# Half of the output projection's inner dimension, multiplied during the threshold search

## The reference

```
sc = indexer_scores(q_idx, w_idx, k_idx)      # one score per query and key
_, idx = lax.top_k(sc, topk)                  # 256 keys per query are attended
a_out = attend(...)                           # 512 rows of the concatenation
s_out, p_out = ssd_mixer(...), pool_mixer(...) # 256 + 256 rows
mix = jnp.concatenate([a_out, s_out, p_out], axis=-1) @ w['w_out']   # 1024 x 1024
x = x + g1 * mix
```

## Time and profile before

| | |
|---|---|
| median of three runs | 3217.33 us |
| span of the profiled execution | 3218.5 us |
| TensorE busy | 3014.0 us, 94% |
| VectorE busy | 1604.0 us, 50% |
| ScalarE busy | 1334.5 us, 41% |
| GpSimd busy | 262.7 us, 8% |
| chain that ended last, by engine | PE 64%, DVE 6%, issue 3%, ACT 2% |
| layer 0's search, layer 1's search | 397 to 556 us, 1975 to 2129 us |
| layer 0's output projection, layer 1's | 761 to 860 us, 2329 to 2431 us |

### The profile page before, as it was taken

One profiled execution on the slowest core, in us unless ns is written; L12 is line 12 of the kernel. 1 busy time (PEld: TensorE's weight loads), 2 busy tenths in 40 slices (PEclk: granted clock), 3 DMA queues, 4 the chain that ended last, 5 costly groups with the idle time before them and its releaser, 6 DMA issues.

```text
span 3218.5 us, 56238 instructions
## 1 busy us (share of the span) xinstructions
PE 3014.0 (94%) x20185; PEld 2635.5 (82%) x20185; DVE 1604.0 (50%) x3493; ACT 1334.5 (41%) x2398; POOL 262.7 (8%) x334
## 2 busy tenths in 40 slices
PE   7999878889999999999989997889899999999998
PEld 5899433558999999999989963346599999999998
DVE  4565699764722322322556567986474222222234
ACT  4433688665522122122443247866564211211234
POOL 1012321011000000000000141100300000000000
PEclk8999989989999999999999998999899999999999
DMA  6622365026311111111432343620642111111124
GB/s 201 163 65 69 108 236 184 2 100 196 99 52 43 48 46 43 48 46 46 116 89 55 69 131 132 209 92 2 230 129 63 45 46 50 46 42 52 46 72 139
DMA packets 356491, 293.60 MB, mean 91 GB/s; under 512 B 85288, under 2 KB 319206, under 8 KB 356024
## 3 DMA queue, kind: packets, MB, share of 16 engines
q1 hardware_dynamic: 325036, 186.21, 19.8%
q0 software_dynamic: 31152, 104.76, 10.5%
q10 hardware_dynamic: 108, 0.11, 0.0%
HBM read 273.33 MB, written 9.78 MB: 88 GB/s over the span
## 4 chain that ended last, share of the span: by engine, by line
PE 64%; DVE 6%; issue 3%; ACT 2%; DMA 1%; POOL 0%; DVEq 0%; ACTq 0%; POOLq 0%; SPq 0%
PE bank L859 44%; PE bank L876 11%; PE bank L843 2%; DVE arena L2635 2%; PE bank L1436 1%; PE bank L1410 1%; DMA arena<-in_cache_v,page_idx 1%; PE bank L917 1%; ACT arena L1902 1%; DVE w_lo L2107 1%; PE bank L1241 0%; PE bank L1370 0%; PE bank L1499 0%; POOL arena L725 0%; ACT w_hi L1629 0%
## 5 line engine op out<-in xcount | busy, mean ns | idle before, releaser
L859 PE MATMUL bank<-h_hi,w_hi 128*128 128x352 f32 x2736 | 891.7, 326 | 11.7 <-DVE arena L2261 7.2
L859 PE MATMUL bank<-h_lo,w_hi 128*128 128x352 f32 x2736 | 880.0, 322 | 0.0
L859 PE MATMUL bank<-h_hi,w_lo 128*128 128x352 f32 x2736 | 879.2, 321 | 0.0
L2107 DVE TENSOR_TENSOR w_lo<-weights,w_hi 128x1024 fp32r<-128x1024 f32 x250 | 306.4, 1225 | 678.0 <-ACT w_hi L1629 671.5
L859 PEld LDWEIGHTS bank<-h_hi,w_hi 128*128 128x128 f32 x2736 | 515.9, 189 | 17.2 <-issue 13.7
L859 PEld LDWEIGHTS bank<-h_lo,w_hi 128*128 128x128 f32 x2736 | 516.5, 189 | 0.3
L859 PEld LDWEIGHTS bank<-h_hi,w_lo 128*128 128x128 f32 x2736 | 515.2, 188 | 0.0
L1629 ACT ACTIVATE w_hi<-weights 128x1024 fp32r<-128x1024 f32 x250 | 264.1, 1056 | 453.3 <-PE bank L859 294.6
L843 PEld LDWEIGHTS bank<-arena 128*128 128x128 f32 (+2 forms) x1717 | 199.3, 148 | 163.3 <-issue 95.3
L843 PE MATMUL bank<-arena 128*128 128x128 f32 (+2 forms) x1717 | 271.1, 290 | 46.1 <-ACT arena L1939 15.8
L876 PE MATMUL bank<-g_hi,w_hi 128*128 128x352 f32 (+2 forms) x768 | 255.7, 333 | 11.1 <-DVE arena L767 5.4
(11 more groups left out here) (396 smaller groups left out, 4369.6 us busy)
## 6 DMA issues: line engine op xcount, KB each, us to landing
arena<-in_w_ada SPq DMA_DIRECT2D x96, 512.0 KB, 4.5
weights<-in_w_down SPq DMA_DIRECT2D x48, 512.0 KB, 3.9
weights<-in_w_gate SPq DMA_DIRECT2D x44, 512.0 KB, 3.8
weights<-in_w_up SPq DMA_DIRECT2D x44, 512.0 KB, 3.8
weights<-in_w_in SPq DMA_DIRECT2D x66, 256.0 KB, 3.8
weights<-in_w_down SPq DMA_DIRECT2D x32, 448.0 KB, 3.6
weights<-in_w_out SPq DMA_DIRECT2D x96, 128.0 KB, 2.9
weights<-in_w_out SPq DMA_DIRECT2D x48, 256.0 KB, 3.1
```

Source lines behind the costliest of these rows:

```text
L859: mm = pe.matmul(bank[:, 0:TC], wt[:, w], xt[:, x], start=(k + m == 0), stop=(k == n_k - 1 and m == 2))
L2107: dve.tensor_tensor(w_lo[:, w], S(O_W + n % 2 * UNIT, UNIT), w_hi[:, w].bitcast(F32), ALU.subtract).then_inc(unit_lo, 1)
```

## The change

For the first two token blocks in layer 0, and the first in layer 1 (`EARLY`), the lower half of the projection (k = 4 to 7, scan and pooling) is multiplied inside the search, in fp32 and without splitting: one product of four matmuls, an output tile m and a token block c, at the end of TensorE's part of every odd pass, from pass 1 in layer 0 (16 products) and from pass 17 in layer 1 (8). SyncE loads the weights of a tile m (256 KB, one buffer) ahead of a pass's `w_ada`. VectorE adds the product to the stream in the next pass, right after its first count (and after `logits_in`, where that pass has it). In the projection the units of those blocks keep k = 0 to 3: two transfers, splits over 512 columns, 12 matmuls. Of the gates, tiles 4 to 7 are rounded only for the blocks that remain.

To make room, ring `A` has two banks in the search, and the outputs of the counts that nobody reads share two buffers per engine, with waits between the counts; key tiles are taken in pairs: in a pass one half of two tiles is transposed, and the two halves of the pass before are multiplied one after the other. The bias of the gate's modulation is added before the search in layer 0, at the first early product in layer 1.

```diff
@@ sizes and places
+EARLY = (2, 1)
+def early_at(l, i):
+    first = 1 if EARLY[l] == 2 else 17
+    if i < first or i % 2 == 0:
+        return None
+    q = (i - first) // 2
+    return q, q // EARLY[l], q % EARLY[l]
+
+def early_base(l):
+    return KD * EARLY[0] * l
-        O_KT = [R(18, 512 * n) for n in range(3)]
-        O_JUNK = R(18, 512 * 3)
+        O_KT = [R(18, 512 * n) for n in range(4)]
+        O_EARLY = R(18, 512 * 4)
+        O_JUNK = (R(18, 512 * 5), R(18, 512 * 5 + 528))
+        O_SIGNS = (R(9), R(18, 512 * 5 + 848))
@@ SyncE
+                def early_unit(m):
+                    if m:
+                        sp.wait_ge(early_done, early_base(l) + EARLY[l] * m)
+                    settle(sp)
+                    sp.dma_start(V(O_EARLY, [[P, 4], [1, P]]), wo[512:1024, m * P:m * P + P].rearrange("(i p) n -> p i n", p=P)).then_inc(early_full, 16)
                 for u in range(4 * KD):
+                    m, rest = divmod(u - (1 if EARLY[l] == 2 else 17), 2 * EARLY[l])
+                    if rest == 0 and m >= 0:
+                        early_unit(m)
                     if u > 1:
                         sp.wait_ge(w_empty, ada_base(l) + u - 1)
...
+                    unit(n, *heads, *(rest if u // KD >= EARLY[l] else ()))
@@ TensorE
-            def product_part(bank, n, x0, wide, hi, lo, used=False, tiles=None, first=0):
-                for k in range(KD):
+            def product_part(bank, n, x0, wide, hi, lo, used=False, tiles=None, first=0, n_k=KD):
+                for k in range(n_k):
...
-                A.restart()
+                A.use(AB_FEW)
...
-                    n, half = h // 2, h % 2
+                    n, half = s // 2 * 2 + j, s % 2
...
+                def key_logits(s):
+                    half = s % 2
+                    A.wait_read(A.count.n - evicted[s])
+                    for i in range(2):
+                        n = s // 2 * 2 + i
+                        gq, j = n // 16, n % 4
+                        if j == 0:
+                            logit_banks[half] = Dr.open()
+                        mm = pe.matmul(B(logit_banks[half], [[1, 512]], 0, 32 * j, 32), S(O_QB + 32 * (4 * gq + j), 32), S(O_KT[(2 * s + i) % 4], 512),
+                                       start=True, stop=True)
+                        if half == 0:
+                            mm.then_inc(s_kv_used, 1)
+                        elif j == 3:
+                            Dr.close_all(mm, 2)
+                def keys(s):
+                    for j in range(2):
+                        keys_turned(s, j)
+                    if s:
+                        key_logits(s - 1)
+                def early_product(i):
+                    if early_at(l, i) is None:
+                        return
+                    q, m, c = early_at(l, i)
+                    if c == 0:
+                        pe.wait_ge(early_full, (l * KD + m + 1) * 16)
+                    if early_base(l) + q:
+                        pe.wait_ge(early_read, early_base(l) + q)
+                    for k in range(4):
+                        mm = pe.matmul(GB[:, 0:TC], S(O_EARLY + P * k, P), S(H(4 + k, c * TC), TC), start=(k == 0), stop=(k == 3))
+                    mm.then_inc(early_done, 1)
                 for i in range(PASSES):
...
                     modulate(O_ADA[i % 2], i % (2 * KD) // 2, i % 2).then_inc(w_empty, 1)
+                    early_product(i)
                 keys(K_TILES - 1)
                 modulation_turn(KD + SEARCH_ROWS[l][1][0])
-                for h in (2 * K_TILES - 2, 2 * K_TILES - 1):
-                    key_logits(h)
+                key_logits(K_TILES - 1)
...
+                                              n_k=4 if c < EARLY[l] else KD))
@@ ScalarE
-                w = slice(n % 2 * UNIT, n % 2 * UNIT + UNIT)
+                w = slice(n % 2 * UNIT, n % 2 * UNIT + wide)
...
-                        junk = S(O_JUNK + 1296 + (S_OFF[j + 2] - S_OFF[5]) // 2, P * (j + 3) // 2).bitcast(BF16)
+                        junk = S(O_SIGNS[j % 2 == 0], P * (j + 3) // 2).bitcast(BF16)
+                        if j == 3:
+                            act.wait_ge(sign_counted, 3 * (l * PASSES + i) + 1)
...
-                split_hi(0, 3)
+                def out_unit(u):
+                    return (2, 4 * P) if u // KD < EARLY[l] else (3, UNIT)
+                split_hi(0, *out_unit(0))
...
-                for k in range(KD):
-                    gate_hi(k, 0, TC)
+                for k in range(4):
+                    gate_hi(k, 0, TC, 1 if k < 3 else KD - 3)
...
-                        gate_hi(k, TC, 2 * TC)
+                        gate_hi(k, *((TC, 2 * TC) if k < 4 else (EARLY[l] * TC, (3 - EARLY[l]) * TC)))
@@ VectorE
+                def early_added(i):
+                    if i < 0 or early_at(l, i) is None:
+                        return
+                    q, m, c = early_at(l, i)
+                    if l and q == 0:
+                        biased(2 * KD, KD)
+                    dve.wait_ge(early_done, early_base(l) + q + 1)
+                    x = S(O_X + m * TOK + c * TC, TC)
+                    dve.scalar_tensor_tensor(out=x, in0=GB[:, 0:TC], scalar=S(O_MOD + 9 * (2 * KD + m), 1), in1=x,
+                                             op0=ALU.mult, op1=ALU.add).then_inc(early_read, 1)
                 def tally(i, sets):
                     for j in sets:
...
+                        junk = S(O_JUNK[j % 2 == 0 and j < 6], n // 2).bitcast(BF16)
+                        if j == 1 and i:
+                            dve.wait_ge(count_raw, l * (PASSES + 1) + (i + 1))
+                        if j == 2:
+                            dve.wait_ge(dve_step, step.count.at(-1))
...
                             if i > 5 and i % 4 == 2:
                                 logits_in((i - 6) // 4)
+                            early_added(i - 1)
...
                 logits_in(7)
+                early_added(PASSES - 1)
...
-                    split_lo(u + 1)
+                    split_lo(u + 1, out_wide(u + 1) if u < 3 * KD - 1 else UNIT)
```

More of the change, by code:

```diff
@@ L875, in product_part @@
                     for m, (wt, xt) in enumerate(((w_hi, hi), (w_hi, lo), (w_lo, hi))):
-                        mm = pe.matmul(bank[:, 0:wide], wt[:, w], xt[:, x], start=(k + m == 0), stop=(k == KD - 1 and m == 2))
+                        mm = pe.matmul(bank[:, 0:wide], wt[:, w], xt[:, x], start=(k + m == 0), stop=(k == n_k - 1 and m == 2))
                         if used and k + m == 0:
@@ L1377, in keys @@
[L1377 to L1382 removed]
+                    evicted[s] = A.count.n
+                def key_logits(s):
[12 more added lines that the diff above has]
+                            Dr.close_all(mm, 2)
@@ L2850, in _, with out_wide @@
                 sample_rows(0)
-                split_lo(0)
-                for k in range(KD):
-                    gate_lo(l, 0, k, 0, TC)
+                def out_wide(u):
+                    return 4 * P if u // KD < EARLY[l] else UNIT
+                split_lo(0, out_wide(0))
+                for k in range(4):
+                    gate_lo(l, 0, k, 0, TC, 1 if k < 3 else KD - 3)
                 sample_rows(1)
```

67 lines of the change are left out of this document (27 added, 40 removed).

## The result

The changed kernel takes 3236.82 us, the median of five executions (3230.91 to 3242.76), against 3217.22 for the kernel before (3209.84 to 3218.4). The ratio is 1.0058, with a 95% interval of 1.0045 to 1.0071: it is slower, by 0.6%. I had said 3220, and 3211 to 3229 for the likeliest case. The wide range went to 3237, so the time lies inside it by 0.2 us. That is luck: the upper end was kept for rivals that did not come, and the forecast of "no change" was wrong by 17 us.

A forecast was written before the change was run, and what follows sets the result against it. TensorE was taken to bound most of the span, with VectorE close behind. Projection -25.5, search +27.5 and bias add +0.4 made +2.4 us: 3221 by the profiled span, stated as 3220 by the median; range 3203 to 3237.

The forecast's parts named there:

- Term -25.5: Projection, both layers: halved units shorten VectorE's turns to 2.66 us, gaining 16.5 us in layer 0 and 9.0 in layer 1.
- Rival 3: Projection: TensorE runs at 1.2 GHz through all short units, 21 us more, 3241; chance 0.05.
- Sum 17.6: Layer 0's search, first pass to last: VectorE's waits and adds, plus passes 1 and 17, cost 17.6 us.
- a wait above 2 us at the add: Search, even passes: forecast wrong if VectorE waits above 2 us at the add; 1.40 was expected in plain passes.
- +27.5: Search of both layers with its ends: early products and adds cost 19.8 us in layer 0 and 7.7 in layer 1.
- 4.5 less 2.2 for pass 1's product: Start of layer 0's search: pass 1's product at half clock costs some 4.5 us, of which 2.2 come back.
- End of the search: Each layer, after the last pass: selection starts 1.65 us later and the last add takes 0.5, 2.15 together.
- The edits costed at nothing: Search: waits for shared discarded-output buffers cost nothing; early weights land in time, with 1 to 2 us slack.
- Rival 1: Search: VectorE's add finds the product done, so the stalls of 14.8 us go, 3205; chance 0.20.
- Rival 2: Search: pairs don't overlap or modulation weights come late, product ends 0.87 us later, 19 more, 3239; chance 0.14.

The follow-up runs named there:

- run 1: Changed kernel with VectorE's add of an early product moved behind all four counts of the even pass, instead of behind the first; 3211.21 us.
- run 2: Changed kernel with only the key-tile pairs and their buffers: no early products in the search, full 24-matmul projection units; 3216.05 us.
- run 11: run 8 plus fourteen dummy fp32 matmuls on TensorE between products 7 and 8 of layer 1's projection; 3205.21 us.
- run 12: run 11 plus dummy matmuls in search passes without early product, four each, eight where logits are evicted; 3206.88 us.
- run 5: Changed kernel plus eight dummy fp32 matmuls on TensorE at the end of every search pass without early product; 3236.49 us.
- run 8: run 1 with layer 0's sixteen early products in a pass list starting at pass 3, so none in pass 1; 3210.28 us.
- Run 9: run 1 with key tiles taken one by one, as in the kernel before, instead of in pairs; 3227.87 us.
- run 10: run 8 with early products and shortened projection in layer 0 only; layer 1 keeps the pairs; 3210.34 us.
- run 7: Changed kernel with the early product placed between the transposes and the logits pair in odd passes; 3232.43 us.

## Why the prediction was right or wrong

**The number.** The forecast was 3220 and the time 3236.82. The forecast meant no change (+2.4), and the kernel became slower by 19.6; the range to 3237 held by 0.2 us only. What follows takes the sum behind the number term by term.

**Projection: right.** Term -25.5, measured -23.9 by the medians. Layer 0, unit 0 to 8: 31.5 before, 21.35 in run 1, forecast 20.7; to unit 16 63.43 and 47.40, 16.0 against 16.5. The changed kernel's own 23.3 is not an error of the turns: its product 0 ran at half clock (3.82 for 12 matmuls). That comes and goes between runs, in full units (65.9 in run 2) and short ones (49.2 in run 11) alike; what decides it I can't say: TensorE's last wait for a value gather was 2.23 us ahead of it in the changed kernel and 2.09 in run 11 (half clock), but 3.85 in run 12 (full). Rival 3 (half clock in all short units) did not come; in layer 1 one unit is hit, the first full-width one, and run 11 shows that its idle wait (3.53 us in the changed kernel) is the cause, worth 2.5 us.

**Search: the step that failed.** As the prediction put it, "In passes with an eviction ahead of the add VectorE comes at 6.48: 0.2 + 0.5 = 0.70. Layer 0 has seven of these (6, 10 to 30) and six plain" and "Sum 17.6". The count of passes and the price of an undisturbed one are right: 5.96 to 6.04, with an eviction or without, against 5.92 and 5.94. What was left out is that the stall itself and the pairs leave TensorE idle 2.3 us before the next count, and that a product at 1.2 GHz then meets VectorE. In the profiled execution passes 12, 14, 22 and 24 cost 14.8 over before, where I had 5.2: 9.6 more. The prediction named a wait above 2 us at the add as a sign that it was wrong, and passes 12, 22 and 24 show 4.51, 2.85 and 2.97. In run 5 these passes are plain ones. By medians the same fill brings nothing although it raises the clock of every execution, so how much of the 19 us between +27.5 and +46.7 is the clock's in an average execution stays open.

I had a rule for it in hand. "TensorE: Matmul & The Clock Gate" of the Trainium skill, section A second HAM failure mode, says that frequent micro-idles between groups of matmuls can make the clock swing. I weighed it against TensorE's pauses of before, 1.4 us at most, and placed it in the projection. After the change the pauses in the search are 2.3 us, and there the trace agrees (0.59, 0.72, 0.57, 0.66). A rule on idle time has to be held against the idle time that the change makes.

**Start of layer 0's search: under-sized.** I had 4.5 less 2.2 for pass 1's product. Passes 2 to 4, less the plain add in pass 4, cost 6.4: 4.1 more. What I had at nothing there is the key tiles' landing behind the early weights, 2.9 us more wait than before; run 8 takes 3.9 off pass 2.

**End of the search: right**, +2.6 and +2.2 against 2.15 each.

**The edits costed at nothing** cost nothing: run 2 has all the new waits for shared buffers and its passes take 4.03 and 5.23 as before. The early weights were on time for all 24 products of the changed kernel, pass 1's too; what they cost is the key tiles' landing at the start.

**Rivals.** Rival 1 (no wait) did not come, but run 1 is it, made by hand: I had 3205 for it, by the sum that mis-sized the rest, and it measured 3211. Rival 2's price (3239) is near the result, but not its mechanism: pairs do overlap. The four instructions of the pair (L1402) start at 448.35 and 448.80, two at a time, and are through by 449.40: 1.05 us, as long as the two instructions of one logits matmul alone. Run 9, which has no pairs and the late add, shows what their lack costs there, some 14 to 17 us.

## What to carry to other kernels

Work that is shifted into another engine's slack is paid for where its result is taken in, and the place of that step in the consumer's queue is a separate decision: one line, moved past 2.2 us of other work, turned +0.6% into -0.2%. Shortening an engine that is not the bound is not free of effect: its longer idle time can cost it its clock, and that shows where something short of slack waits for it. Price each half alone: layer 1's half brought nothing by the medians (run 10), and even with its own clock fall filled it brings some 3 us in the traces (run 11 against run 10: 8.4 off the projection, 5.5 onto the search).

## What the runs showed of the hardware

- Dummy matmuls held the granted clock at 1.00 in a wait of 3.7 us that otherwise ended at 0.50, for 3.3 us of matmul work whose output nobody reads, and unit 8 to unit 9 was 2.5 us shorter (run 11).
- In the 55 us of the earlier trace rows TensorE waited 11 times for the count, 1.4 us at most, and the clock stayed at 1.00; with pauses of 2.3 us it fell at some and not at others: between 436 and 468 us of the changed kernel there are four of them and the window has 0.99. In layer 0 of run 7 there are seven pauses of 2.8 us, and the clock fell at all seven.
- One kernel's executions spread over 7 to 16 us; the mean granted clock over the span is 0.955 to 0.971 in all of them together, and in every kernel here the executions with a higher one tend to be shorter (run 1: 0.966 and 3199.55, 0.960 and 3215.72). A few microseconds in one profiled trace are not yet a difference of kernels: run 5's trace shows 9 us that its median doesn't.
